# Expert matrices in whole 32 KB rows, one go of up products for each quad, and own buffers for the second matrices

## What is computed

```
def hier_moe(h, w_group, b_group, w_expert, b_expert, w_in, w_out):
    ...   # 4 groups of 8 experts; top-1 group, top-2 experts in it, for each token
    def expert_block(args):
        xb, e = args
        hu = xb @ w_in[e]                                   # 1024 x 1024
        return (jax.nn.silu(hu[:, :EXPERT_FF]) * hu[:, EXPERT_FF:]) @ w_out[e]   # 512 x 1024
    ...
    y = y_buf[dest] * flat_w[order][:, None].astype(y_buf.dtype)
    out = jnp.zeros_like(ht).at[token_of].add(y)
```

## Time and profile before

| | |
|---|---|
| median of 3 runs | 1167.5 us (1167.28 to 1168.05) |
| the profiled execution | 1167.82 us, of which the span of the trace is 1166.0 us |
| TensorE matmuls busy | 866.5 us (74%), mean granted clock 0.875 |
| VectorE, ScalarE busy | 269.6 us, 132.5 us |
| DMA | 447.76 MB, mean 384 GB/s, SP's queue 92.1% of the 16 engines' time |

### The profile page before, as it was taken

How to read it: one execution, slowest core, us unless ns; L and a number is a source line. 1 busy time by engine, 2 the same in 40 slices (tenths; PEclk the granted TensorE clock), 3 DMA queues, 4 the chain that set the end, 5 groups by cost and what they waited for, 6 DMA issues and landing times.

```text
span 1166.0 us, 12503 instructions
## 1 busy us (share of the span) xinstructions
PE 866.5 (74%) x5238; PEld 412.6 (35%) x5238; DVE 269.6 (23%) x504; ACT 132.5 (11%) x328; POOL 24.0 (2%) x27
## 2 busy tenths in 40 slices
PE   9999999946566655656689999986565656565666
PEld 7965655312121212222234565532222222222222
DVE  3565673010101010101038746301010101010102
ACT  2011211100000000000011241110000000000000
POOL 1000110000000000000002100000000000000000
PEclk9999999977878787878899999998788887877789
DMA  9985588999999999999999937899999999999997
GB/s 351 281 323 211 216 319 329 422 428 428 429 427 428 430 427 428 428 427 429 415 410 405 377 145 286 317 428 427 429 426 428 428 428 429 427 428 427 427 420 294
DMA packets 51817, 447.76 MB, mean 384 GB/s; under 512 B 4496, under 2 KB 6840, under 8 KB 26936
## 3 DMA queue, kind: packets, MB, share of 16 engines
q1 hardware_dynamic: 49696, 444.43, 92.1%
q10 hardware_dynamic: 2072, 2.62, 1.2%
HBM read 444.41 MB, written 2.62 MB: 383 GB/s over the span
## 4 chain that ended last, share of the span: by engine, by line
DMA 45%; PE 45%; SPq 5%; issue 2%; DVE 1%; ACT 1%; POOL 0%; DVEq 0%; POOLq 0%
PE ps L1394 44%; DMA ring<-in_moe_w_in 29%; DMA ring<-in_moe_w_out 15%; SPq L466 3%; SPq L372 2%; DMA ring<-in_w_kv 1%; PE ps L1397 1%; DMA xs<-const_turned 0%; ACT ps L668 0%; DVE work L1141 0%; ACT work L638 0%; DVE work L1274 0%; SPq L500 0%; DVE work L1225 0%; ACT work L664 0%
## 5 line engine op out<-in xcount | busy, mean ns | idle before, releaser
L1394 PE MATMUL ps<-ring,work 128*32 128x512 f32 (+1 forms) x3360 | 602.6, 694 | 272.4 <-DMA ring<-in_moe_w_in 149.0
L1394 PEld LDWEIGHTS ps<-ring,work 128*32 128x32 f32 (+1 forms) x3360 | 190.8, 135 | 621.7 <-issue 605.0
L1214 DVE SCALAR_TENSOR_TENSOR work<-work,ps 128x512 f32<-128x512 f32 x16 | 11.0, 688 | 678.5 <-ACT work L699 678.5
L1394 PE MATMUL ps<-work 128*128 128x128 f32 (+4 forms) x498 | 127.5, 437 | 3.0 <-ACT work L706 1.6
L1394 PEld LDWEIGHTS ps<-work 128*128 128x128 f32 (+2 forms) x498 | 64.1, 176 | 62.1 <-issue 59.1
L638 ACT ACTIVATE work<-ps,first 128x128 f32<-128x128 f32 x120 | 34.3, 369 | 272.0 <-PE ps L1394 272.0
L1394 PEld LDWEIGHTS ps<-work,xs 128*128 128x128 f32 x512 | 58.8, 192 | 15.1 <-issue 15.1
L1394 PE MATMUL ps<-work,xs 128*128 128x128 f32 x512 | 62.8, 279 | 0.0
L706 ACT COPY work<-ps 128x512 f32<-128x512 f32 x32 | 18.8, 586 | 316.2 <-PE ps L1394 316.2
L1394 PE MATMUL ps<-work,ring 128*128 128x128 f32 (+1 forms) x352 | 53.3, 313 | 0.3 <-DVE work L817 0.3
L1394 PEld LDWEIGHTS ps<-work,ring 128*128 128x128 f32 x352 | 49.3, 191 | 4.5 <-issue 0.6
(11 more groups left out here) (155 smaller groups left out, 347.8 us busy)
## 6 DMA issues: line engine op xcount, KB each, us to landing
ring<-in_moe_w_in SPq DMA_DIRECT2D x112, 2048.0 KB, 20.0
ring<-in_moe_w_out SPq DMA_DIRECT2D x50, 2048.0 KB, 19.6
ring<-in_moe_w_in SPq DMA_DIRECT2D x22, 1024.0 KB, 16.4
ring<-in_hg_w_in SPq DMA_DIRECT2D x7, 2048.0 KB, 20.3
ring<-in_moe_w_out SPq DMA_DIRECT2D x24, 512.0 KB, 14.3
work<-in_moe_w_out SPq DMA_DIRECT2D x4, 2048.0 KB, 9.9
ring<-in_moe_w_in SPq DMA_DIRECT2D x12, 512.0 KB, 7.4
ring<-in_w_kv SPq DMA_DIRECT2D x3, 2048.0 KB, 24.9
```

The lines of the kernel that those rows point to most:

```text
L1214: dve.scalar_tensor_tensor(en, en, 1.0, ps[:, 6, :], ALU.add, ALU.mult).then_inc(silu_ready, 1)
L1394: return pe.matmul(o, l, r, start=start, stop=stop)
```

## The change

- A first matrix is one DMA of 4 MB with 32 KB a partition (rows 8p to 8p+7) into a pair of ring slots (`pair`); the ring holds the four first matrices of a quad.
- The second matrices have four buffers of their own, `down_home`, throughout (the former `extra`). `y`, `hid` and `xgT` shrink into `region(2)` to make room: one `xgT` instead of two, `hid` over `y`, and no `en`: tanh and both silu steps work in place in `hid`, in the transposed layout.
- The up products of a quad are one go, and SP loads the next four first matrices behind `up_done` of all of it. The next gather follows the whole go. The first quad still starts with row blocks 0 to 3, the last in three parts.
- The opening: `load_opening`; the pair that the out projection's weights occupy (`SPLIT_PAIR`) comes in two halves. The first refill (`load_refill`) is one DMA with row 0 of four experts behind the first row block, then rows 1 to 3 behind the fourth block, then rows 4 to 7 behind `up_done`.
- The residual's columns are in the order 8q + k over the whole width. The out projection and layer 0's down products therefore read 4 of every 8 columns (`out_quarter`, `down_half`), keys, queries and values are loaded with 16 KB rows 32 KB apart.
- Layer 0's last row block of second matrices comes whole, and both down halves go before the first combine. Before, the two halves were loaded and multiplied one after the other; in layer 1 they still are.

```diff
 QUADS = E // GRP
-QC = 3 * GRP
-EXTRAS = 4
 RING = 8
 SPARE = 3
-EXTRA_HOME = {RING: 0, RING + 1: 1, 0: 2, RING + 2: SPARE}
 UN = 2
 ITERS = QUADS // UN
-TURNS = QC * UN // RING
 MAXPASS = T // CAP
-MIX0, MOE0 = 0, 10
-MIX1 = MOE0 + QC * QUADS - EXTRAS
-MOE1 = MIX1 + 8
-MOE = [MOE0, MOE1]
+MIX0, MIX1 = 0, 2 * RING
+SPLIT_PAIR = (0, GRP - 1)
+ROW_PARTS = (GRP + 1, 2 * GRP)
 NR = 3 * P
 KQ_SUMS, KQ_COPIED = (14, 21), (3, 6)
...
-        x_out = region(6).rearrange("p (a n) -> p a n", n=D)
+        x_out = ring[:, 0, 0:TT * D].rearrange("p (a n) -> p a n", n=D)
...
-        xgT = region(2).rearrange("p (b k s) -> p b k s", b=2, s=P)
-        y = region(1)[:, 0:1024]
-        en = region(1)[:, 1024:1536]
-        hid = region(1)[:, 1536:2048]
+        xgT = region(2)[:, 0:1024].rearrange("p (k s) -> p k s", s=P)
+        y = region(2)[:, 1024:2048]
+        hid = y[:, 0:FF]
...
-        extra = [region(6, 2), region(3, 2), region(0, 2), spare[:]]
+        down_home = [region(6, 2), region(3, 2), region(0, 2), spare[:]]
...
+        def down_half(layer, c, k, half):
+
+            if layer == 0:
+                return c.rearrange("p (k q e) -> p k q e", k=KF, e=KD)[:, k, :, half * 4:(half + 1) * 4]
+            return down_view(c)[:, k, half * 512:(half + 1) * 512]
...
-            return w[half * 512:(half + 1) * 512, :].rearrange("(p k) n -> p k n", k=KD // 2)
+            return w.rearrange("(p h k) n -> p h k n", h=2, k=KD // 2)[:, half]
...
+        def out_quarter(c, j, half):
+
+            return rows_view(chunk(c + j)).rearrange("p k (q e) -> p k q e", e=KD)[:, :, :, half * 4:(half + 1) * 4]
...
+            def up_matrix(layer, e):
+                return moe_w_in[layer, e].rearrange("(p k) n -> p (k n)", k=KD)
...
+                def load_pair(e, x, signal, ks=(0, KD)):
+                    ns = slice(ks[0] * D, ks[1] * D)
+                    sp.dma_start(pair(x)[:, ns], up_matrix(layer, e)[:, ns]).then_inc(signal, 16)
+
+                def load_down(e, x):
+                    sp.dma_start(down_view(down_home[x]), down_rows(moe_w_out[layer, e])).then_inc(down_in[x], 16)
+
+                def load_opening():
+                    first_slot = MIX1 if layer else MIX0
+                    if layer:
+                        sp.wait_ge(down_done, 2 * QUADS)
+                        load_down(SPARE, SPARE)
+                    for x in range(GRP):
+                        if x != split:
+                            sp.wait_ge(*read(first_slot + 2 * x))
+                            sp.wait_ge(*read(first_slot + 2 * x + 1))
+                            load_pair(x, x, loaded[2 * x])
+                    if layer == 0:
+                        sp.wait_ge(pred_done, LEVELS + 1)
+                        load_down(SPARE, SPARE)
+                        sp.wait_ge(o_done, 4)
+                        sp.wait_ge(og_ready, 2 * TT)
+                    else:
+                        sp.wait_ge(pv_done, 4)
+                        sp.wait_ge(mx_ready, H)
+                    for x in range(SPARE):
+                        if layer == 0 and x == 2:
+                            sp.wait_ge(ot_done, 2 * TT)
+                        load_down(x, x)
+                    out_slot = MIX1 + 6 if layer else MIX0 + 8
+                    sp.wait_ge(sums_ready, OUT_SUMS[layer] + 7)
+                    for half in range(2):
+                        sp.wait_ge(*read(out_slot + half))
+                        load_pair(split, split, loaded[2 * split + half], (half * KD // 2, (half + 1) * KD // 2))
...
+                def load_refill():
+                    sp.wait_ge(first_k_done, 2 * layer + 1)
+                    sp.dma_start(ring[:].rearrange("p (x s) n -> p x (s n)", s=2)[:, :, 0:D],
+                                 moe_w_in[layer, GRP:2 * GRP].rearrange("x (p k) n -> p x k n", k=KD)[:, :, 0, :])\
+                      .then_inc(row_part_in[0], 16)
...
+                    sp.wait_ge(first_k_done, 2 * layer + 2)
+                    for x in range(GRP):
+                        load_pair(GRP + x, x, row_part_in[1], (1, KD // 2))
+                    sp.wait_ge(up_done, 2 * P0 + 2)
+                    for x in range(GRP):
+                        load_pair(GRP + x, x, loaded[2 * x], (KD // 2, KD))
+
+                def body(it):
+                    for u in range(UN):
+                        if is_int(it, 0) and u == 0:
+                            load_opening()
+                            continue
+                        e0 = it * (GRP * UN) + u * GRP
+                        if is_int(it, 0):
...
+                            load_refill()
...
+                            sp.wait_ge(up_done, it * (2 * UN) + 2 * (P0 + u))
+                            if last_quad(it, u):
+                                load_last_up()
+                                load_last_down()
+                                continue
+                            for x in range(GRP):
+                                load_pair(e0 + x, x, loaded[2 * x])
...
+                        sp.wait_ge(down_done, it * (2 * UN) + 2 * (P0 + u))
...
+                            load_down(e0 + x, x)
+
+                def load_last_up():
+                    for part, ks in enumerate(((0, 4), (4, 6), (6, 8))):
+                        for x in range(GRP):
+                            load_pair(E - GRP + x, x, loaded[2 * x] if part == 2 else row_part_in[part], ks)
...
+                def load_last_down():
+                    sp.wait_ge(down_done, 2 * (P0 + QUADS - 1))
+                    parts = [(k, slice(0, D)) for k in range(KF)]
+                    if layer:
+                        parts[KF - 1:] = [(KF - 1, slice(0, 512)), (KF - 1, slice(512, D))]
...
-                    dve.scalar_tensor_tensor(en, en, 1.0, ps[:, 6, :], ALU.add, ALU.mult).then_inc(silu_ready, 1)
+                    dve.scalar_tensor_tensor(hid_rows, hid_rows, 1.0, in_hidden(6), ALU.add, ALU.mult).then_inc(silu_ready, 1)
                     dve.wait_ge(silu_ready, it * UN + (q + 1))
                     dve.wait_ge(up_done, it * (2 * UN) + (2 * q + 2))
-                    if not (type(it) is int and it * UN + q < 1):
-                        dve.wait_ge(ht_done, it * UN + q)
-                    dve.scalar_tensor_tensor(hid_rows, en.rearrange("p (q k) -> p q k", k=KF), 0.5,
-                                             ps[:, 7, :].rearrange("p (q k) -> p q k", k=KF), ALU.mult, ALU.mult)\
+                    dve.scalar_tensor_tensor(hid_rows, hid_rows, 0.5, in_hidden(7), ALU.mult, ALU.mult)\
...
+            def up(gate_up, ks):
 
                 for k in ks:
                     for x in range(GRP):
                         rows = slice(x * BLK, (x + 1) * BLK)
-                        i = mm(ps[rows, 6 + gate_up, :], xgT[:, buf, 4 * half + k, rows],
-                               rows_view(weights[x])[:, k, gate_up * 512:(gate_up + 1) * 512],
-                               half == 0 and k == 0, half == 1 and k == KD // 2 - 1)
+                        i = mm(ps[rows, 6 + gate_up, :], xgT[:, k, rows],
+                               rows_view(pair(x))[:, k, gate_up * FF:(gate_up + 1) * FF], k == 0, k == KD - 1)
...
-                                    i = up(group(r), 0, 0, gate_up, [k])
-                                if k < 2:
+                                    i = up(gate_up, [k])
+                                if k in (0, KD // 2 - 1):
...
+                            split = SPLIT_PAIR[layer]
+                            pe.wait_ge(loaded[2 * split + 1], 16 * (loads(MIX1 + 2 * split + 1) + 1 if layer else 3))
+                            pe.wait_ge(xg_ready, 2 * q + 2)
+                            for gate_up in range(2):
+                                up(gate_up, range(KD // 2, KD)).then_inc(up_done, 1)
...
+                                    up(gate_up, range(KD)).then_inc(up_done, 1)
...
-                        down(group(r), 0, [KF - 1]).then_inc(down_done, 1)
-                        combine(it, u, 0, 0, False, True)
-                        group_in(r)
-                        down(group(r), 1, [KF - 1]).then_inc(down_done, 1)
+                        down(layer, down_home, 0, [KF - 1]).then_inc(down_done, 1)
+                        if layer == 0:
+                            down(layer, down_home, 1, [KF - 1]).then_inc(down_done, 1)
...
-        return a.reshape(*a.shape[:-1], 2, P, 4).swapaxes(-1, -2)
+        return a.reshape(*a.shape[:-1], P, KD).swapaxes(-1, -2)
```

300 lines of the change are left out of this document (107 added, 193 removed).

## The result

The changed kernel took 1173.13 us, median of 5 executions (1172.21 to 1174.48), against 1167.58 us (1167.28 to 1168.05) for the kernel before: ratio 1.0047, 95% interval 1.0033 to 1.0062. It is slower by 5.6 us. The forecast was 1165.3 us with a range to 1171.0; the result lies outside it, on the side of rival (b). Measured once more in a later series the unaltered kernel took 1174.91 us (1173.04 to 1178.39), ratio 1.0061 (1.0047 to 1.0076). It spans 2.3 and 5.4 us in the two series, the kernel before 0.8 and 2.9: a first hint that something in it comes out differently in each execution.

What follows compares the result with a forecast made beforehand. The prediction took two weight streams, bound by bytes over DMA rate, and engine chains between them as the bounds. Its terms, -3.5 + 0 + 1.3 + 0 = -2.2 us, gave a median of 1165.3 us, range 1162.3 to 1171.

Steps and rivals of the forecast that it cites:

- rival (b): Queue runs dry behind the downs in every quad: 2.4 to 12 us added, some 1172 us; chance 0.15.
- Step 1: Expert streams, quads 2 to 6: 32 KB rows raise the DMA rate from 428 to 431.8 GB/s, -3.5 us.
- (a): Expert streams: longer rows bring nothing, the DMA being held by something independent of rows; 1168.8 us, chance 0.15.
- (c): Expert streams: rows 32 KB apart run into each other in memory; 1177 us, chance 0.05.
- (d): Rate reaches 433 GB/s or over and the first refill costs nothing: -5 us, 1162.5; chance 0.10.
- Step 2: Gaps between quads: queue refilled after 18.9 us where 19.6 are covered, so 0 us; upper end 12 us in all.
- two lag rows: Lone 2 MB DMAs, 7.6 and 8.5 us from issue to landing, 4.9 of it bytes: lag 2.7 to 3.6 us.
- Step 3: First refill of each stream: later refills put it 0.65 us behind, +1.3 us in both layers.
- Step 4: Layer 0's end: last downs in one piece, first key product +1.3 us, third waits anyway; 0, bounds -0.3 and +1.5.

Runs made afterwards that it cites:

- `short_go`: Changed kernel with row 3 left out of the up products of quads 1 to 6 (112 records, not 128), all bytes still loaded: 1167.57 us.
- `rows16_short`: Changed kernel with quads 2 to 6's first matrices in 16 KB rows and row 3 left out of the up products of quads 1 to 6: 1170.45 us.
- `before_one_piece`: Kernel before, with layer 0's last row block waited for whole and both down products done ahead of the first combine: 1170.17 us.
- the dose runs: Changed kernel with the up go shortened by leaving out products (1167.57 us), or its signal delayed by small matmuls (1191.79 us); unaltered 1174.91 us.
- `late_go`: Changed kernel with eight small matmuls between the last up product and its signal in quads 1 to 6: 1191.79 us.
- `warm`: Changed kernel with 94 small matmuls while TensorE waits for the first matrices of quads 2 to 6, both layers: 1178.38 us.
- `warm2`: Changed kernel with 84 small matmuls in the first quad of a loop turn and 110 in the second, ahead of the up go: 1176.07 us.

## Why the forecast was wrong

The mechanism that sets the time (bytes over rate, plus gaps, plus the two ends) was right, and each place was named. Two of the four terms, the hand-overs and layer 0's end, were put at nothing and cost microseconds; the other two came out near their size:

| step | forecast | measured |
|---|---|---|
| 1 rate of 32 KB rows | -3.5 | -2.9 (`short_go` against `rows16_short`) |
| 2 hand-overs | 0 | +7.3 (unaltered against `short_go`) |
| 3 first refill | +1.3 | +1.4 against before (profiles); +4.4 against what it could be |
| 4 layer 0's end | 0 | +2.4 (`before_one_piece`) |
| sum | -2.2 | +8.2; the kernel itself +5.6 and +7.4 |

**Step 1** held. The period of a quad without a gap is 58.45 us with 32 KB rows and 58.8 with 16 KB; 0.35 for 16.78 MB is the 3.5 us of the sum. Rivals (a), (c) and (d) are out: the rate rose; 16 KB rows 32 KB apart (`rows16_short`, about 58.8 us a period) went as fast as in the kernel before (58.77); and the rate stayed within the bounds, with the refill not free.

**Step 2** failed, and it carries the result. The go had its forecast length. The step that failed is "I take 16.2 + 2.7 = 18.9 us, 0.7 us to spare, and 0": the wait at the hand-over, put at nothing, measured 7.3 us, 0.6 for each of twelve. Two things were wrong in it. First, it took the lower of two lag rows, 2.7 us, with the reason that a running queue has no start to make; the dose runs put the lag at about 3.4 us on average, near the other row's 3.6. Second, it compared a mean with a limit. The mean go was 16.0 us in one profiled execution and 15.8 in the other. With a lag of 3.4 even that corrected sum has 0.2 to 0.4 us to spare and gives no cost, yet 0.6 us a time was paid. A hand-over that falls short costs time, and one with time to spare gives nothing back, so the mean of the costs is not the cost of the mean. The go varies from 15.2 to 16.9 us, and `late_go` shows the limit itself varying by 1.5. The go's length alone doesn't say which hand-over is dear: goes of 15.28 and 15.30 us were followed by stretched periods, one of 16.86 by none. What varies besides the go stays open. The text held rival (b) possible at 0.15 and priced it at 2.4 to 12 us; the measured 7.3 lies in the middle. The upper bound of the term, 12 us, should have been part of the range.

**Step 3** was right in size against before: 0.6 us in layer 0 and 0.8 in layer 1 (783.40 - 738.24 = 45.16 us before, 789.38 - 743.46 = 45.92 after). But the size is in part luck. The text halved between two cases, 257 GB/s without a pause (0.9 us) and 411 GB/s with a pause (0.4); the run was the second, 417 GB/s from 183 to 187 us and a share of 0.61 from 186 to 190, and it cost 0.6 to 0.8. What the text did not see is that the kernel before had a loss in the same place.

**Step 4** had +1.3 us at the first key product and then let a wait of 0.97 us swallow it. The product came 2.7 us later: the eight groups behind the last landing ran at the lower clock, 3.5 us in place of 1.7. What the wait could not take, 2.7 - 0.97 = 1.7 us, went on down the chain: 1.5 at the third key product, 1.4 at the next refill. The bound of +1.5 counted no lower clock. Of the 2.4 us in the medians 1 stays unexplained. In the changed kernel itself the last row block stands 8.0 us ahead of the first key product, as in `before_one_piece` (8.1).

The measured terms add to 8.2 us, the kernel to 5.6 and 7.4 in two series; with a scatter of 2 to 5 us in the kernel itself that is as close as these runs can close it.

## What to carry to other kernels

When a transfer queue is refilled behind a computation, don't compare means with what is still queued. Compute the shortfall of each case, the longest with the largest lag included: a shortfall costs time and slack is not refunded, and here 0.2 to 0.4 us to spare on average still lost 7.3 in twelve hand-overs. Where an engine is idle anyway, let it do the work in a form that takes longer but releases part of the buffers early; here two goes of half the width, each as long as one, gave back 7 us. And where the first refill of a stream begins, look for a pause in the first microseconds: taking it out was worth 4.4 us, more than the whole rate gain.

## What the runs showed of the hardware

- A granted clock of 1.00 ahead of a go does not mean that the go keeps it: after 5.0 us without work it was still 1.00 when the go began and fell to 0.50 (1.2 GHz) within it (windows of `warm`).
- Rows of 32 KB: a quad of 25.17 MB, two thirds of it in 32 KB rows and one third in 16 KB rows, takes 58.45 us, so 430.6 GB/s; all in 16 KB rows 58.8 us, 428.
- A row block of all four pairs as one DMA of 2.1 MB in 4 KB rows, followed by the next, moved 367 GB/s in the first 6 us, where DMAs of 0.5 MB in 4 KB rows moved 257.
- Behind a loop turn (quads 4 and 6) TensorE stood 3.6 to 5.4 us "<-issue" before its next matmul (`warm`, `warm2`).
